# Leaving out the products of the identity with itself in a two-model float32 forward pass

## What the reference computes

```python
for layer in range(DEPTH):                       # first block, DEPTH = 2
    h = hybrid_mixer(x, ...)                     # gated mixer
    x = layer_norm(DEEPNORM_ALPHA * x + h, ...)
    f = swiglu(x, ...) if layer % 2 == 0 else moe_swiglu(x, ...)
    x = layer_norm(DEEPNORM_ALPHA * x + f, ...)

def moe_swiglu(x, w_router, e_gate, e_up, e_down):   # 8 experts, 2 a token, hidden width 3584
    logits = t @ w_router
    top_val, top_idx = lax.top_k(logits, TOP_K)
    ...
    for e in range(N_EXPERTS):
        out = out + gates[:, e:e + 1] * swiglu(t, e_gate[e], e_up[e], e_down[e])

for i in range(DEPTH):                           # second block
    y = swiglu_2(x, ...);  x = layer_norm_2(ALPHA * x + 0.5 * y, ...)
    y = mixer_ab(x, ...) if i % 2 == 0 else mixer_c(x, ...)
    x = layer_norm_2(ALPHA * x + y, ...)
    y = memory_attn(x, mem, ...);  x = layer_norm_2(ALPHA * x + y, ...)
    y = swiglu_2(x, ...);  x = layer_norm_2(ALPHA * x + 0.5 * y, ...)
```

## Time and profile before

| | |
|---|---|
| median of 3 executions | 2540.68 us (2540.28 to 2542.49) |
| the profiled execution's own time | 2539.72 us |
| its span, first to last instruction | 2538.5 us |
| PE busy | 2503.4 us (99%) |
| PE weight loads busy | 1775.7 us (70%) |
| DVE busy | 1053.2 us (41%) |
| ACT busy | 819.4 us (32%) |
| POOL busy | 142.2 us (6%) |
| read from HBM | 637.72 MB |
| mean granted TensorE clock | 0.999 |

### The profile page before, as it was taken

One profiled execution on the slowest core, in us unless ns is written; L12 is line 12 of the kernel. 1 busy time (PEld: TensorE's weight loads), 2 busy tenths in 40 slices (PEclk: granted clock), 3 DMA queues, 4 the chain that ended last, 5 costly groups with the idle time before them and its releaser, 6 DMA issues.

```text
span 2538.5 us, 40504 instructions
## 1 busy us (share of the span) xinstructions
PE 2503.4 (99%) x18081; PEld 1775.7 (70%) x18081; DVE 1053.2 (41%) x1486; ACT 819.4 (32%) x1134; POOL 142.2 (6%) x144
## 2 busy tenths in 40 slices
PE   9999999999999999999999999999999999999998
PEld 7899885444444444444446997798997998789897
DVE  6755562010101010010115557847556555766654
ACT  5444342110101101010113444744443443645442
POOL 2200130000000000000000001000000003400000
PEclk9999999999999999999999999999999999999999
DMA  7565468999999999999995645356655646265651
GB/s 276 198 223 192 155 218 332 370 361 385 377 357 375 388 376 356 377 388 366 377 335 184 200 150 182 110 182 210 200 178 191 200 158 232 100 206 181 221 186 53
DMA packets 335238, 641.51 MB, mean 253 GB/s; under 512 B 15700, under 2 KB 128512, under 8 KB 334672
## 3 DMA queue, kind: packets, MB, share of 16 engines
q1 hardware_dynamic: 330208, 618.64, 68.4%
q0 software_dynamic: 4848, 20.20, 2.3%
HBM read 637.72 MB, written 1.05 MB: 252 GB/s over the span
## 4 chain that ended last, share of the span: by engine, by line
PE 91%; DVE 4%; POOL 2%; DMA 1%; ACT 1%; issue 1%; SPq 0%; DVEq 0%
PE bank L620 16%; PE bank L622 16%; PE bank L621 16%; PE bank L1364 15%; PE bank L1378 8%; PE bank L1411 8%; PE bank L1433 4%; PE bank L1049 1%; PE bank L1396 1%; DVE part_lo L568 1%; PE bank L1020 1%; POOL bias L2748 1%; DMA turned_raw<-in_w_in_dram 1%; PE bank L632 1%; POOL bias L2750 1%; PE bank L1350 1%
## 5 line engine op out<-in xcount | busy, mean ns | idle before, releaser
L568 DVE TENSOR_TENSOR part_lo<-raw,part_hi 128x2048 fp32r<-128x2048 f32 x149 | 339.6, 2294 | 160.0 <-ACT part_hi L560 160.0
L620 PE MATMUL bank<-x_hi,turned_part_hi 128*128 128x256 f32 x1440 | 401.5, 279 | 0.0
L621 PE MATMUL bank<-x_lo,turned_part_hi 128*128 128x256 f32 x1440 | 398.8, 277 | 0.0
L622 PE MATMUL bank<-x_hi,turned_part_lo 128*128 128x256 f32 x1440 | 398.7, 277 | 0.0
L560 ACT ACTIVATE part_hi<-raw 128x2048 fp32r<-128x2048 f32 x149 | 281.5, 1908 | 17.1 <-DMA raw<-in_mem_w_kv_dram 10.4
L620 PEld LDWEIGHTS bank<-x_hi,turned_part_hi 128*128 128x128 f32 x1440 | 270.7, 188 | 6.0 <-issue 2.7
L621 PEld LDWEIGHTS bank<-x_lo,turned_part_hi 128*128 128x128 f32 x1440 | 271.0, 188 | 3.2
L622 PEld LDWEIGHTS bank<-x_hi,turned_part_lo 128*128 128x128 f32 x1440 | 270.5, 188 | 0.0
L568 DVE TENSOR_TENSOR turned_part_lo<-turned_raw,turned_part_hi 128x2048 fp32r<-128x2048 f32 x98 | 224.3, 2321 | 88.5 <-ACT turned_part_hi L560 87.2
L620 PE MATMUL bank<-part_hi,x_hi 128*128 128x512 f32 x528 | 210.5, 399 | 8.5 <-DVE part_lo L568 5.9
L1364 PE MATMUL bank<-raw,expert_in 128*64 128x512 f32 x896 | 214.1, 598 | 0.0
(11 more groups left out here) (274 smaller groups left out, 3485.1 us busy)
## 6 DMA issues: line engine op xcount, KB each, us to landing
raw<-in_exp_w_gate_dram SPq DMA_DIRECT2D x112, 512.0 KB, 6.3
raw<-in_exp_w_up_dram SPq DMA_DIRECT2D x112, 512.0 KB, 7.7
raw_hi<-in_exp_w_gate_dram SPq DMA_DIRECT2D x112, 512.0 KB, 8.1
raw_hi<-in_exp_w_up_dram SPq DMA_DIRECT2D x112, 512.0 KB, 9.3
raw<-in_exp_w_down_dram SPq DMA_DIRECT2D x56, 1024.0 KB, 12.8
raw_hi<-in_exp_w_down_dram SPq DMA_DIRECT2D x56, 1024.0 KB, 14.3
raw<-in_ffn_w_down_dram SPq DMA_DIRECT2D x55, 1024.0 KB, 5.0
turned_raw<-in_ffn_w_gate_dram SPq DMA_DIRECT2D x70, 512.0 KB, 4.2
```

Source lines behind the costliest of these rows:

```text
L568: p.nc.vector.tensor_tensor(p.part_lo[t][i][:, :], p.raw[t][i][:, :], p.part_hi[t][i][:, :].bitcast(F32), ALU.subtract).then_inc(*self.spl ...
L620: nc.tensor.matmul(out, stat_hi, move_hi, start=start, stop=False, skip_group_check=True)
L621: nc.tensor.matmul(out, stat_hi, move_lo, start=False, stop=False, skip_group_check=True)
L622: return nc.tensor.matmul(out, stat_lo, move_hi, start=False, stop=stop, skip_group_check=True)
```

## The change

All calls of `pe_meanwhile` and the function itself are left out: 7 + 7 in the rotated mixer, 12 + 4 + 8 + 4 around the router, 2 + 8 + 3 at the ends of the experts. That is 55 products of the path that runs, 110 instructions. Nothing is added or reordered.

```diff
-def pe_meanwhile(p, bank, n):
-
-    for _ in range(n):
-        p.nc.tensor.matmul(p.bank[bank][:, 0:P], p.const("identity"), p.const("identity"), start=True, stop=True,
-                           skip_group_check=True)
@@ pe_ab
     scores(0)
-    pe_meanwhile(p, 7, 7)
     scores(1)
-    pe_meanwhile(p, 7, 7)
     scores(2)
     turn(0)
@@ pe_router
         if tt:
-            pe_meanwhile(p, 5, 12)
             pe_turn_rows(p, st - 1, 1)
-            pe_meanwhile(p, 5, 4)
...
     out = p.bank[5]
-    pe_meanwhile(p, 5, 8)
     pe.wait_ge(*p.g.at("before_me"))
     pe.wait_ge(*p.v.at("routed"))
@@ pe_experts
     pe_four_down(p, st, last, frees=False)
     pe_pair_down(p, st, last, frees=True)
-    pe_meanwhile(p, 4, 2)
     pe_scatter_last(p, count - 1)
@@ experts_again
     held = p.first_loads[st][:2 * RING]
-    pe_meanwhile(p, 6, 4)
     pe_gather(p, 0)
@@ build_program
     pe_experts(p, moe, N_EXP, begun=True)
-    pe_meanwhile(p, 4, 8)
     pe_turn_rows(p, moe, 0, (0,))
-    pe_meanwhile(p, 4, 3)
     pe_turn_rows(p, moe, 0, (1,))
```

## The result

The changed kernel takes 2546.05 us in the median of 18 executions, the kernel before 2539.60 in the median of 18 that were timed beside it. The ratio is 1.0024, with a 95% interval of 1.0018 to 1.0030: slower by 6.1 us (4.6 to 7.6); the two medians are 6.45 us apart. The profiled execution took 2546.08 us. The forecast was 2546.2.

What follows compares the result with a forecast made beforehand. The prediction took PE, with 91% of the chain of waits, to bound the kernel. Terms -0.4 + 2.6 + 2.0 + 1.3 = +5.5 us on 2539.72, plus 0.96 for the median, gave 2546.2 us; range 2541.0 to 2551.5.

Steps and rivals of the forecast that it cites:

- Direct part: All places: fillers gone from PE's queue let the router's transposes start 0.37 us earlier, term -0.4 us; other places 0.
- The clock: Router, ends of the experts, rotated mixer: idle PE lets the granted clock fall, +2.6, +2.0 and +1.3 us; chance 0.65.
- Rival 1: All three places: the clock holds, or almost; 2540.3 us without a dip, 2542.3 with one at the experts' ends; chance 0.17.
- the border between 2.30 and 2.66 us: Single PE waits in the trace before: 2.30 us passed without a dip, 2.66 us brought one; border not sharp.
- Rival 3: All places: faster by more than 5 us, needing at least 44 of 110 instructions directly ahead of ready work; chance 0.04.
- Rival 2: Router: clock stays low until the gather or `pe_pair_up` has run a while, 8 instead of 2.6 us, 2551.6 us; chance 0.14.
- router, low clock: Router to gather: small products and count 0.9 us slower, about half the gather low 1.7; together +2.6 us, bounds 0 to 8.
- ends of the experts: Behind the scatter: one dip over the first transposes (+0.4) and most of 1.6 us in dense products; +2.0, bounds 0 to 3.3.
- rotated mixer: Between the first scores: one group at half speed, +1.0 us, later slowness partly hidden by a wait; +1.3, bounds 0 to 4.
- I take a third: Router, small products and count: a third of the 2.5 us that doubling would cost, 0.9 us, as part runs at full clock.
- The 0.96 us that I added for the median: Whole kernel: the profiled execution, 2539.72 us, lay 0.96 us below the median of three, 2540.68, so 0.96 was added.
- The signs that the prediction named: Changed profile: clock below 1.00 at three places, transposes 0.4 us earlier, pair up to 2 later, dense 0.4, third scores 1.

Runs made afterwards that it cites:

- e10: Kernel before plus 11 fillers at the 1933 us wait, 9 ahead of the branch, 29 tiny products at the start; router's 12 cut to 10; 2539.68 us.
- e12: Kernel before plus 11 fillers at the 1933 us wait and 38 tiny products at the start; router's 12 cut to 10; 2539.03 us, ratio 0.9996.
- e8: Kernel before with 4 fillers behind the scatter left of the 2, 8 and 3 at the ends of the experts; 2542.10 us, ratio 1.0007.
- e11: Kernel before with about half of each filler group (router 6, 2, 4, 2; ends 1, 4, 1; mixer 3, 3); 2540.41 us, ratio 1.0004.
- e1: Kernel before without the 28 fillers around the router (12, 4, 8 and 4); 2540.26 us, ratio 1.0001.
- e6: Kernel before without the router's 28 fillers, with 28 tiny products in a wait at the start; 2541.09 us in one execution.
- e13: Kernel before without its small filler groups (4, 4, 2, 3); the 12, 8, 8, 7, 7 in the long waits stay; 2539.52 us, ratio 1.0003.
- e3: Kernel before without the 14 fillers in the rotated mixer (7 and 7); 2543.19 us, ratio 1.0012.
- e2: Kernel before without the 13 fillers at the ends of the experts (2, 8 and 3); 2542.40 us, ratio 1.0009.
- e9: Kernel before plus 11 fillers ahead of the 2.66 us wait at 1933 us; 2539.22 us, ratio 0.9996.
- e4: Kernel before with 14 instead of 4 fillers ahead of the router's gather; 2540.43 us, ratio 1.0001.
- e7: Kernel before with all its fillers, plus 36 tiny products in a wait at the start; 2538.38 us, ratio 0.9997.

## Why the prediction was right

**Direct part.** Predicted -0.4 at the router and 0 elsewhere. The transposes start 0.38 us earlier, once the 0.48 by which all is late there is taken off; e10 and e12 show 0.38 and 0.37 for two fillers fewer. At the end of the experts the second transposes come 0.5 us earlier and nobody gains by it, as argued. Right.

**The clock.** Predicted to fall at all three places; it does, in every profile taken with no filler there: three at the router, two at the ends, two in the mixer. Rival 1 fell: e8 has a dip with 1.90 us as its longest wait, e11 one at the router with 0.96. So does the border between 2.30 and 2.66 us that the prediction drew from one trace. The Trainium skill ("TensorE: Matmul & The Clock Gate", "Why this matters for your kernels") advises against idle gaps over about 3 us between bursts of products; these two traces show that keeping to this isn't enough here. Rival 3, a gain, fell. Rival 2 was half right, the one that I had given 0.14: the router did stay low until two thirds of the gather were over (13.6 us), but the wait behind the branch took up most of the price. That the clock came down wherever the fillers were missing bears out the mechanism as predicted. One part of it is narrower than I put it: a row of waits isn't always needed. In e1 and e6 the clock fell 0.9 and 1.4 us into the router's first wait, with only the 16 small products of tokens 0 to 127 just ahead of it.

Two readings of the trace before were off, and nothing hung on them. The clock is also low from 2534.6 us on, when the last product has long been done. And the prediction puts the gather at 396.15, where the earlier trace rows have 396.52.

**The sizes.** Here the terms missed, and the nearness of 2546.2 to 2546.05 is in part luck:

| term | predicted | measured in the changed kernel |
|---|---|---|
| router, low clock | +2.6 | +3.9 to the pair, +0.9 behind the branch's waits |
| ends of the experts | +2.0 | +2.7 |
| rotated mixer | +1.3 | +2.9 |
| direct | -0.4 | -0.4 |
| sum | +5.5 | +6.4 in the traces (a dip by chance at the start is 0.5 of it) |

At the router the term had two parts. The gather's was right: 1.7 predicted, 1.7 measured (the pair's 3.5 us less 1.8 at the gather's start). The part ahead of it was not: 0.9 predicted, 2.2 measured. "I take a third" failed for the small products: they doubled (16 in 1.81 us before; a pair of them 0.43 us apart instead of 0.22 here), and the transposes, left out of this part, added 0.4. And the sum passed over a row that it had in hand, the wait of 2.30 us ahead of 409.65: I used it only as a witness on the clock, and not as a cover for what goes ahead of it. At the ends the prediction priced one dip, 3.4 us, over the transposes and the first dense products. The clock was low for 6.8 us, from the first dense product on, so nothing was lost at the transposes and 2.7 us in the dense products. In the mixer both later groups of scores ran low, not one. The chain from scores to DVE to scores passed that on, and the wait of 1.42 us took back little.

The 0.96 us that I added for the median had no ground: over 18 executions the kernel before has 2539.60, next to its profiled execution's 2539.72. It made up for most of what the sum lacked: 5.5 predicted, 6.45 between the medians (6.1 by the ratio). The signs that the prediction named came out in part. The clock, the transposes, the third scores (0.9 us later against the first; 1 expected) and the stretches between the places did; to the pair it was 3.5 us, not "up to 2", and from the scatter to the first dense product 0.0, not 0.4.

## What to carry to other kernels

Before you take filler products out, or put them in, list the waits of TensorE in a row, not one by one: in the mixer the two waits of 1.7 us, with 1 us of work between, brought a dip in both traces that have them, while the single wait of 2.3 us did so in 3 of 7. Waits of 0.8 to 1.0 us are the open ground: in a row they brought a dip at e11's router, and none at e13's ends of the experts (0.78, 1.01 and 0.84 us). Then look at what stands behind: a dip costs only where a dense or chained stretch follows, and nothing where a wait behind it takes up the delay. And book by place, product by product; a total of a quarter of a per cent hid one place that cost 0.5 us and two that cost 5.6.

## What the runs showed of the hardware

- Small products follow the clock too: with 16 and 8 columns they stand 0.11 us apart at 1.00 and 0.21 at 0.50, transposes likewise.
- Where the clock falls differs from trace to trace of the same row of waits: at the router within the first wait (e1, e6) or just behind it (changed kernel), in the mixer within the first wait (changed kernel) or the second (e3).
- The same wait of 2.66 us has a dip in some executions and none in others (6 of 11 traces); the wait at the branch, where it was 2.3 us or more, has one in 3 of 7 (e2, e8, e9). One dip costs 1.0 us at the branch and 1.6 at 1933 us, so chance dips would explain a part of the differences between executions of one kernel: of the kernel before, those with a mean clock of 0.999 took 2536.7 to 2540.1 us, those with 0.997 2540.6 to 2543.4.
- The wait behind the branch: in all 14 traces the first product comes 2.4 to 3.0 us after the start of a transfer of 16 KB on the queue that the profile calls "instruction" (by the trace's DMA records), also in the three where it comes directly behind the last product ahead of the branch. A pair that is late by 1.7 or 1.8 us (e4, e11, e13) moves that transfer by 0.2 us at most. One that is late by 3.5, 4.5 and 4.7 us (changed kernel, e1, e6) moves it by 0.9, 1.8 and 2.1: there it starts 2.3 us ahead of the start of the last product before the branch. Fillers directly ahead of the branch move it by 1.4. Why, stays open. The second wait changed with the branch's place in the stream (0.47 us before, 0 in e7), which is what fetching by blocks would give; that it is the cause is argued, not shown.
